# State products of eight running streams: 32 stationary columns, four streams side by side, another order of streams

## The reference, cut to what matters

```python
s = einsum('bthd,bshd->btsh', q, k) * exp(dmat - m_t)
num = einsum('btsh,bshe->bthe', s, v) + w_inter * einsum('bhed,bthd->bthe', c_st, q)
...
c_new = w_c * c_st + einsum('bsh,bshe,bshd->bhed', w_s, v, k)
```

## Time and profile before

| what | us |
|---|---|
| median of three runs | 2829.86 |
| the profiled execution | 2829.37 |
| its span | 2827.6 |
| PE busy | 2751.4 (97%) |
| DVE, POOL, ACT busy | 1039.7, 866.1, 531.6 |
| steps of heads 0, 1, 2 (L953 first to L999 last) | 1390.2 to 1478.8, 1537.8 to 1626.5, 1685.4 to 1774.1 |
| steps of the last head | from 1833.0 |

### The profile page before, as it was taken

How to read it: one execution, slowest core, us unless ns; L and a number is a source line. 1 busy time by engine, 2 the same in 40 slices (tenths; PEclk the granted TensorE clock), 3 DMA queues, 4 the chain that set the end, 5 groups by cost and what they waited for, 6 DMA issues and landing times.

```text
span 2827.6 us, 38099 instructions
## 1 busy us (share of the span) xinstructions
PE 2751.4 (97%) x15795; PEld 2670.4 (94%) x15795; DVE 1039.7 (37%) x1390; ACT 531.6 (19%) x910; POOL 866.1 (31%) x729
## 2 busy tenths in 40 slices
PE   7999999999999999999999999989999999999997
PEld 7997689999999999999889898979999999999997
DVE  5217825222222222257646464553522212212214
ACT  3113712110010001022322223131300100100112
POOL 6543422222222222223122222252222222222222
PEclk9999989999999999999999999999999999999998
DMA  6320021111111111121232232432111111111111
GB/s 191 72 55 28 4 97 45 38 45 45 37 45 45 37 45 45 37 104 52 47 93 55 74 78 62 90 114 105 45 38 45 45 37 44 45 37 45 45 38 75
DMA packets 107106, 164.01 MB, mean 58 GB/s; under 512 B 55564, under 2 KB 66828, under 8 KB 106240
## 3 DMA queue, kind: packets, MB, share of 16 engines
q1 hardware_dynamic: 33088, 103.67, 12.0%
q10 hardware_dynamic: 73648, 57.98, 7.2%
q0 software_dynamic: 272, 0.98, 0.1%
HBM read 132.81 MB, written 24.49 MB: 56 GB/s over the span
## 4 chain that ended last, share of the span: by engine, by line
PE 92%; DVE 4%; issue 2%; ACT 1%; POOL 1%; DMA 0%; ACTq 0%; POOLq 0%; DVEq 0%
PE psum L620 77%; PE psum L941 4%; PE psum L719 2%; PE psum L647 1%; PE psum L983 1%; PE psum L1023 1%; PE psum L1017 1%; PE psum L973 1%; PE psum L800 1%; DVE low L1448 1%; DVE low L1452 1%; PE psum L841 1%; PE psum L965 0%; PE psum L953 0%; PE psum L817 0%
## 5 line engine op out<-in xcount | busy, mean ns | idle before, releaser
L445 POOL TENSOR_SCALAR w_hi<-w_raw 128x1024 fp32r<-128x1024 f32 x191 | 203.8, 1067 | 1602.9 <-PE psum L620 1291.1
L620 PE MATMUL psum<-a_hi,w_hi 128*128 128x384 f32 x2808 | 652.6, 340 | 27.2 <-DVE a_lo L1090 16.8
L620 PE MATMUL psum<-a_lo,w_hi 128*128 128x384 f32 x2808 | 640.1, 335 | 0.0
L620 PE MATMUL psum<-a_hi,w_lo 128*128 128x384 f32 x2808 | 639.2, 335 | 0.0
L620 PEld LDWEIGHTS psum<-a_hi,w_hi 128*128 128x128 f32 x2808 | 499.4, 189 | 35.2 <-issue 23.7
L620 PEld LDWEIGHTS psum<-a_lo,w_hi 128*128 128x128 f32 x2808 | 502.5, 188 | 0.0
L620 PEld LDWEIGHTS psum<-a_hi,w_lo 128*128 128x128 f32 x2808 | 502.3, 188 | 0.0
L448 POOL TENSOR_TENSOR w_lo<-w_raw,w_hi 128x1024 fp32r<-128x1024 f32 x191 | 460.8, 2413 | 15.9
L1124 DVE TENSOR_TENSOR low<-psum,low 128x1152 f32<-128x1152 f32 x143 | 194.1, 1357 | 622.3 <-PE psum L620 622.2
L620 PE MATMUL psum<-h_hi,w_hi 128*128 128x384 f32 x1536 | 348.4, 334 | 0.0
L620 PE MATMUL psum<-h_hi,w_lo 128*128 128x384 f32 x1536 | 348.4, 334 | 0.0
(11 more groups left out here) (230 smaller groups left out, 2247.7 us busy)
## 6 DMA issues: line engine op xcount, KB each, us to landing
w_raw<-in_wall SPq DMA_DIRECT2D x191, 512.0 KB, 3.3
low<-in_x ACTq DMA_DIRECT2D x16, 576.0 KB, 9.0
high<-in_mem_in ACTq DMA_DIRECT2D x32, 257.0 KB, 4.7
out_mem_s<-high ACTq DMA_DIRECT2D x32, 257.0 KB, 3.2
out_x_spill<-low ACTq DMA_DIRECT2D x8, 576.0 KB, 2.7
low<-out_x_spill ACTq DMA_DIRECT2D x8, 576.0 KB, 7.1
out_mix_spill<-mid ACTq DMA_DIRECT2D x3, 1152.0 KB, 4.5
back<-out_mix_spill ACTq DMA_DIRECT2D x3, 1152.0 KB, 7.6
```

Source lines behind the costliest of these rows:

```text
L445: nc.gpsimd.tensor_scalar(w_hi[:, s, :], w_raw[:, s, :], 1.0, 1.0, ALU.mult, ALU.mult)\
L620: r = mm(psum[:, z + i, 0:TN], w[:, s, k * P:(k + 1) * P], a[:, kk, tok(i)], start=first and n == 0, stop=last and n == 2)
```

## The change

Streams are renumbered by `ORDER`: the even ones first. The state products leave `stream` and go to `read_states(g)`, called in step 0 (streams 0, 2, 4, 6) and step 6 (1, 3, 5, 7): for each of the two key halves, four matmuls of 32 stationary columns, whose outputs go to four quarters of the bank's partitions. Stream 2j+g has the 16 columns from 16g of quarter j, and zeros in the other 16. The increments are dealt out anew: one stream each in steps 0 and 1, two each in steps 2, 6 and 7, none in steps 3, 4, 5 and 8.

```diff
-STREAMS = [[b] for b in range(NLC - 2)] + [[NLC - 2, NLC - 1], [], []]
+ORDER = [0, 2, 4, 6, 1, 3, 5, 7]
+STREAMS = [[0], [1], [2, 3], [], [], [], [4, 5], [6, 7], []]
+READ_AT = {0: 0, 6: 1}
...
-        qx = take(2, NB, P)
+        qx = take(2, NB, 2 * TB)
...
+                def read_states(g):
+
+                    for j in range(NCS):
+                        pe.wait_ge(cs_in[j], 16 * CS_USES * h + 16 * (g + 1))
+                    for k in range(2):
+                        for j in range(NCS):
+                            r = mm(psum[2 * TB * j:2 * TB * (j + 1), STREAM_BANK, 0:MA], qx[:, k, ORDER[NCS * g + j], :],
+                                   csl[:, j, MA * k:MA * (k + 1)], start=g == 0 and k == 0, stop=g == 1 and k == 1)
+                    if g:
+                        r.then_inc(ab_done, 1)
+
                 def stream(b, c, first):
 
-                    s = b % NCS
-                    pe.wait_ge(cs_in[s], 16 * CS_USES * h + 16 * (b // NCS + 1))
-                    for k in range(2):
-                        r = mm(psum[:, STREAM_BANK, 0:MA], qx[:, k, b, :], csl[:, s, MA * k:MA * (k + 1)],
-                               start=b == 0 and k == 0, stop=b == NB - 1 and k == 1)
-                    if b == NB - 1:
-                        r.then_inc(ab_done, 1)
                     pe.wait_ge(kwm_done, 8 * h + (b + 1))
-                    if first:
+                    if first and c < NLC:
                         pe.wait_ge(cu_done, 9 * h + (c + 2))
                     else:
                         pe.wait_ge(csu_done, 8 * h + (b + ONE))
...
-                        if c >= 1:
-                            pe.wait_ge(csu_done, 8 * h + (min(c + (c == NLC - 1), NB) + ONE))
+                        updated = sum(len(at) for at in STREAMS[:p])
+                        if updated:
+                            pe.wait_ge(csu_done, 8 * h + (updated + ONE))
...
+                    if p in READ_AT:
+                        read_states(READ_AT[p])
...
-                for b in range(NB):
-                    r = V.tensor_copy(qx[:, :, b, TB * b:TB * (b + 1)], mq[:, :, TP + TB * b:TP + TB * (b + 1)])
+                for g in range(2):
+                    r = V.tensor_copy(
+                        qx.rearrange("p k (j g) t -> p k j g t", g=2)[:, :, :, g, TB * g:TB * (g + 1)],
+                        mq[:, :, TP:T].rearrange("p k (j g t) -> p k j g t", g=2, t=TB)[:, :, :, g, :])
...
-                    dma(csl[:, s, :], t["mem_in"][h, b]).then_inc(cs_in[s], 16)
+                    dma(csl[:, s, :], t["mem_in"][h, ORDER[b]]).then_inc(cs_in[s], 16)
```

More of the change, by code:

```diff
@@ L1526, in updated @@
                     m = csl[:, s, :].rearrange("p (k e) -> p k e", k=2)
-                    V.scalar_tensor_tensor(out=m, in0=m, scalar=wch[:, 8 + b:9 + b], in1=psum[:, 4:6, 0:MA],
+                    V.scalar_tensor_tensor(out=m, in0=m, scalar=wch[:, 8 + ORDER[b]:9 + ORDER[b]], in1=psum[:, 4:6, 0:MA],
                                            op0=ALU.mult, op1=ALU.add).then_inc(csu_done, 1)
@@ L1940, in masked_keys @@
                         act.wait_ge(csc_done, 8 * h + (b - 1))
-                    A(kwm[:, b % 2, :], ks, ACT.Copy, scale=ws8[:, b:b + 1]).then_inc(kwm_done, 1)
+                    A(kwm[:, b % 2, :], ks, ACT.Copy, scale=ws8[:, ORDER[b]:ORDER[b] + 1]).then_inc(kwm_done, 1)
                 def sample_out(b):
@@ L1945, in sample_out @@
                     act.wait_ge(csu_done, 8 * h + (b + 1 + ONE))
-                    dma(t["mem_s"][h, b], csl[:, s, :]).then_inc(cs_out[s], 16)
+                    dma(t["mem_s"][h, ORDER[b]], csl[:, s, :]).then_inc(cs_out[s], 16)
                 def ogate(m):
```

## The result

Six runs of the changed kernel took 2843.26 us in the median (2841.46 to 2844.24), six of the kernel before 2830.01 (2828.82 to 2835.05): ratio 1.0046, interval 1.0035 to 1.0056, so 13.2 us slower. The forecast was 2842, in a range of 2835 to 2852. The profiled execution took 2843.43 with a span of 2841.6, 14.1 more than the profiled one before.

The account below looks back on a forecast made before the run. The bound was taken as the PE, DVE, PE wait chain, not PE's turns. Heads 0 to 2 +10.9, last head +2.9, memset -1.3, copies -0.1: +12.4 us, so 2842 in the median, range 2835 to 2852.

Parts of the forecast that it names:

- Products: Narrow products in steps 0 and 6: PE runs out at each tile-shape change, +0.2 us at each of two places.
- the rival built on it: Narrow tiles run one after the other, steps 0 and 6 cost 2.4 more each: 2859, half overlap 2850; chance 0.12.
- Step 1: The product goes, but L983 stays 1.97 after the start of L1023: 0.
- Step 2: A second stream's increment waits for the first one's way through DVE: +2.04 us.
- Steps 3 to 5: Without increments, L999 waits for L1494, at X+2.41 (X: start of L1023) instead of X+2.91: 0.50 less each, -1.50.
- Step 6: Two streams before and after: 0, apart from the products.
- Step 7: Two increments before L999 where PE waited; the second delays L965 of the following step: +2.69 us.
- A head: Sum of the step terms for one of heads 0 to 2: +3.63 us, 10.9 for the three.
- Last head: POOL's splittings absorb the middle steps; 0.2 from the first step's products and 2.69 from the late increments remain: +2.9 us.
- The clock is the rival: PE's clock falls after the late waits in each head, at most 1.7 us each: 2849; chance 0.12.
- Before the heads: DVE's memset of `qx` falls from 2048 columns to 512, shortening PE's wait of 9.09: -1.27 us.
- The copies: Eight copies become two before L1462, which waits for PE's unit anyway: -0.1 us for all heads.

Follow-up runs that it names:

- one-product: Kernel before with only stream 7's state product issued, the other seven streams' products left out: 2833.39 us, ratio 1.001.
- step-3 kernels: Changed kernel with stream 3's state increment moved back from step 2 to step 3: 2839.76 us, ratio 1.0030 to the kernel before.
- stream 7 in step 8: Changed kernel with stream 7's increment moved into the middle of step 8's filler: 2841.42 us, ratio 1.0037 to the kernel before.
- the wide memset: Changed kernel with the memset before the first head widened to 2048 columns again: 2843.39 us in one run.
- busy work: Changed kernel with unused matmuls added in PE's waits of the last head's steps 3 to 7: 2842.72 us, ratio 1.0044 to the kernel before.
- the first filler: Changed kernel with each step's 24 filler matmuls moved behind L1031, in parts around the streams, step 0 included: 2826.34 us, ratio 0.9984 to the kernel before.
- with filler: Filler matmuls moved behind the prompt's increment from step 1 on, step 0 unchanged: in the changed kernel 2806.37 us, in the kernel before 2818.04.

## Why the prediction was right

The time came out 1.3 above the forecast, and the mechanism is the one forecast, but two terms of the sum were off in opposite directions: heads 0 to 2 by 1.7 too much, the last head by 3.1 too little. That they partly cancel is luck, and so is what the clock did at four places, none of them in the sum.

*Products.* 0 instead of 0.2 a place. The block starts 0.96 after L1031 instead of 0.87, so the change of shape costs about 0.1, and its 16 instructions start 0.046 apart. The drain at a change of mode of which the Trainium skill tells ("TensorEngine Tiling (Array Packing)", "Key Properties") fits these 0.09, but they are hidden. The last turn ends at about 1398.66, before L1550 does at 1398.78. I had added the run-out to a term that had 0.23 of slack, and to a block of 0.87 where 16 x 0.046 = 0.74 are seen. The 16 loads take 0.59 beside running matmuls. The rule of the Trainium skill that loads overlap only where the row groups differ ("TensorE: Matmul & The Clock Gate", "The mechanism" in Part 3) is not borne out for column tiles here either, and the rival built on it is out. The loads alone would not show that: at full width too they run beside matmuls (PEld is busy 93% of the span, PE 96%). It is the 0.046 that shows four tiles side by side.

*Steps 1 to 6.* Step 1: 0. Step 2: +2.05 (L990 to L990) for 2.04. Steps 3 to 5: L1006 at X+2.41 (1426.60 to 1429.01), 0.50 less each in steps 3 and 4, 0.48 in step 5. Step 6: +0.03. Each as forecast, and the one-product and step-3 kernels show why: what PE is relieved of in a wait is not given back.

*Step 7.* +2.52 for 2.69. L1539 started 0.08 before L1516 had ended, a small overlap that I had priced at zero, and the step's chain follows L1539. The kernel with stream 7 in step 8 confirms that the second increment carries it.

*A head* is thus 3.02 to 3.09 longer, not 3.63: 9.2 for three heads instead of 10.9.

*Last head.* +6.0 where 2.9 was forecast: the mis-sized term. I had said that POOL absorbs steps 2 to 5, so that the first increment of step 6 stays where it was. Counted from the head's start, step 7 does begin only 0.15 later, but that is luck. In step 6, against the earlier trace rows:

```profile
1890.92 2.63 POOL L585 TENSOR_TENSOR a_lo<-back,a_hi 128x1152 fp32r<-128x1152 f32 x1
...
1897.06 1.13 PE L990 MATMUL psum<-high,kwm 128*128 128x257 f32 x4
```

POOL's splitting starts 49.89 after the head's start instead of 49.00, and the increment 56.03 instead of 54.91, 1.12 later. From there to step 7 it is 5.16 instead of 6.14: the kernel before had a fall of the clock in this stretch, and the kernel after had its own earlier in the step. The end was off too. Before and after in the timeline, steps 7 and 8, before:

```profile
1892.93 2.62 POOL L582 TENSOR_TENSOR a_lo<-back,a_hi 128x1152 fp32r<-128x1152 f32 x1
1893.83 1.87 DVE L1509 TENSOR_SCALAR mid<-mid 128x256 f32<-128x256 f32 x1
1894.06 0.67 PE L965 MATMUL psum<-high,mid 128*128 128x257 f32 x2 [0.57 <-DVE mid L1518]
...
1897.68 0.67 PE L965 MATMUL psum<-high,mid 128*128 128x257 f32 x2 [0.79 <-DVE mid L1518]
```

and after:

```profile
1901.86 2.61 POOL L585 TENSOR_TENSOR a_lo<-back,a_hi 128x1152 fp32r<-128x1152 f32 x1
1902.00 2.63 DVE L1521 TENSOR_SCALAR mid<-mid 128x256 f32<-128x256 f32 x1
1902.22 0.67 PE L968 MATMUL psum<-high,mid 128*128 128x257 f32 x2 [0.57 <-DVE mid L1530]
...
1906.59 1.64 PE L990 MATMUL psum<-high,kwm 128*128 128x257 f32 x4 [2.83 <-DVE high L1539]
...
1909.68 1.20 PE L968 MATMUL psum<-high,mid 128*128 128x257 f32 x2 [1.03 <-DVE mid L1530]
```

Step 7 grew by 3.83. From the start of L968 to the end of the held-up L1521 it is 2.41 instead of 1.64 (L965 to L1509's end): +0.77. From there to step 8's L968 it is 5.05 instead of 1.98, +3.07; of that 0.53 is the clock (L990 to L968 takes 3.09, in head 0 2.56), and 2.54 is the change itself, close to its 2.69. Step 8 grew by 2.05, with 0.51 granted over 6.8 us; at the full clock, with the wide memset, it took 3.30 as before. So at the end 2.6 are the clock, 2.5 the change, and 0.8 is L1521, held up beside POOL. The clock is the rival that I had given 12%, come true in the last head alone, and there dearer than the 1.7 that I had put as its most.

*Before the heads.* PE's wait fell by 0.9 (9.09 to 8.18 in the rows), not by 1.27. In all 1.95 was gained there. The other 1.0 is the clock and not the change: from the end of this wait to the first head it is 41.43 us instead of 42.46, with 0.85 granted in the first 10 us instead of 0.74. Other kernels with the small memset and the same code up to there took 41.35 and 41.38 at 0.85, but 42.49 and 42.82 at 0.73 and 0.70 (busy work and stream 3 in step 3; stream 7 in step 8 and the first filler). The copies gave 0.08 in each head (start column), 0.3 in all for the 0.1 forecast.

The profiled sum: 9.2 + 6.0 - 1.95 = 13.3, and 0.8 more from a fall of the clock in the attention near 275 us, which this profile has, as most others do, and that of the kernel before does not: 14.1.

## What to carry to other kernels

A matmul whose turn ended inside a semaphore wait cost nothing here, and taking it out gained nothing: look at what the next instruction waits for before counting turns, and count the waits that the new order adds. Narrow tiles were faster only side by side, and the change paid only once other work filled the waits that it left (2843 against 2830 alone, 2806 against 2818 with filler). Filler belonged behind the instruction whose result DVE has to take out, and not where its absence opens a new wait, as in step 0. And a profile is one execution: before a term is compared with it, look at where the clock fell in each of the two.

## What was not expected of the hardware

- Sixteen matmuls of 32 stationary columns and 257 moving ones take 1.07 us with their run-out, 0.046 apart, against 0.217 for full width: more than four to one. On one quarter alone, four of them take 1.05.
- PE's clock fell to its lower level, 1.2 GHz, after stretches in which PE waited, at a cost of 1.5 to 2 us in a step 8, but not at the same places in each run: head 0's step 8 was 6.55 in the kernel after and 8.23 with the wide memset.
- The DVE instruction L1521 (128x256) takes 0.35 in step 3 of head 0; in the last head it took 2.63 beside a POOL instruction of 2.61, and ended 0.16 after it. The Trainium skill has a rule for this ("SBUF — State Buffer", "Who interferes with whom"): DVE and POOL share a pair of ports, and when a DVE instruction uses both of its ports, whichever comes first holds the pair for a whole instruction and the other waits. The rows agree with that: L1521 began 0.14 after POOL's instruction and ended 0.16 after it.
